# Latent attention with values as weights and probabilities scaled ahead of their transposes

## The reference

```python
def conv_attn_mixer(xn, w_in, conv_w, conv_b, conv_ln_g, conv_ln_b,
                    q_norm, kv_norm, w_uq, w_ukv, w_out):
    ...
    u = jax.nn.silu(layer_norm(u, conv_ln_g, conv_ln_b))
    ...
    q_nope, q_rope = q[..., :QK_NOPE_DIM], rope(q[..., QK_NOPE_DIM:], pos)
    kv = (rms_norm_2(c_kv, kv_norm) @ w_ukv).reshape(b, s, N_HEADS, QK_NOPE_DIM + V_HEAD_DIM)
    k_nope, v = kv[..., :QK_NOPE_DIM], kv[..., QK_NOPE_DIM:]
    k_rope = rope(k_r[:, :, None, :], pos)[:, :, 0, :]
    attn = mla_attention(q_nope, q_rope, k_nope, k_rope, v)
    return jnp.concatenate([u, attn], axis=-1) @ w_out
```

## Time and profile before

| | us |
|---|---|
| median of 3 runs | 2614.75 |
| the profiled execution, its own time | 2618.45 |
| its span, first to last instruction | 2616.0 |
| TensorE matmuls busy | 2539.7 (97%) |
| TensorE weight loads busy | 1748.8 (67%) |
| VectorE busy | 1303.1 (50%) |
| ScalarE busy | 640.2 (24%) |
| the units of the latent attention, first transposes to second half of the projection | 1553.48 to 1623.80 |

### The profile page before, as it was taken

The page is one execution under the profiler, slowest core; times in us unless marked ns, Lnnn a source line. Parts: engine busy times, 40 slices in busy tenths (PEclk is TensorE's granted clock), DMA queues, the critical chain, the costliest instruction groups (busy, mean ns, idle before and its releaser), DMA issues.

```text
span 2616.0 us, 38542 instructions
## 1 busy us (share of the span) xinstructions
PE 2539.7 (97%) x15741; PEld 1748.8 (67%) x15741; DVE 1303.1 (50%) x2873; ACT 640.2 (24%) x1168; POOL 329.5 (13%) x315
## 2 busy tenths in 40 slices
PE   8999998999999999999999999999999999999998
PEld 4766756777775684444444446688864575888887
DVE  2244565757632251000035845676765675777733
ACT  1156643323430222110011144212110122121201
POOL 0222115445441400000001000000000000000000
PEclk9999999999999999999999999999999999999999
DMA  4211111111113232444413110222223212222222
GB/s 188 77 63 49 49 56 58 39 45 52 49 50 138 88 109 81 167 171 161 174 67 113 65 48 33 89 81 97 81 97 112 97 35 81 84 94 81 95 83 80
DMA packets 32520, 227.41 MB, mean 87 GB/s; under 512 B 3552, under 2 KB 4192, under 8 KB 6112
## 3 DMA queue, kind: packets, MB, share of 16 engines
q1 hardware_dynamic: 30384, 219.50, 23.5%
q10 hardware_dynamic: 1968, 5.51, 0.6%
HBM read 222.90 MB, written 2.10 MB: 86 GB/s over the span
## 4 chain that ended last, share of the span: by engine, by line
PE 90%; DVE 4%; ACT 3%; issue 2%; POOL 1%; DMA 0%; ACTq 0%; DVEq 0%; POOLq 0%
PE psum L404 88%; PE psum L907 1%; DVE work L1613 0%; ACT work L970 0%; PE psum L2977 0%; PE psum L2638 0%; ACT work L3031 0%; PE psum L1262 0%; ACT work L968 0%; ACT work L976 0%; ACT L976 0%; ACT work L988 0%; DVE work L1920 0%; POOL ring L1455 0%; POOL ring L1438 0%
## 5 line engine op out<-in xcount | busy, mean ns | idle before, releaser
L404 PE MATMUL psum<-hT,ring 128*128 128x256 f32 (+2 forms) x2872 | 542.8, 370 | 4.0 <-issue 1.7
L404 PEld LDWEIGHTS psum<-hT,ring 128*128 128x128 f32 (+1 forms) x2872 | 371.9, 161 | 135.7 <-issue 94.0
L404 PE MATMUL psum<-work,ring 128*128 128x256 f32 (+1 forms) x1176 | 378.0, 472 | 4.6 <-ACT work L3903 2.4
L404 PEld LDWEIGHTS psum<-work,ring 128*128 128x128 f32 x1176 | 222.0, 190 | 144.3 <-issue 121.6
L404 PE MATMUL psum<-xT,ring 128*128 128x256 f32 (+2 forms) x1184 | 293.1, 400 | 15.6 <-POOL ring L1438 7.1
L404 PE MATMUL psum<-work,mixT 128*128 128x256 f32 (+2 forms) x1332 | 289.3, 379 | 1.2 <-DVE mixT L4118 0.7
L404 PEld LDWEIGHTS psum<-work,mixT 128*128 128x128 f32 (+1 forms) x1332 | 232.1, 182 | 47.7 <-issue 16.3
L404 PE MATMUL psum<-work 32*32 32x32 f32 (+8 forms) x5374 | 255.5, 248 | 8.4 <-issue 3.7
L404 PEld LDWEIGHTS psum<-work 32*32 32x32 f32 (+5 forms) x5374 | 210.5, 124 | 78.0 <-issue 51.9
L404 PEld LDWEIGHTS psum<-xT,ring 128*128 128x128 f32 (+1 forms) x1184 | 211.0, 188 | 71.2 <-issue 25.7
L404 PE MATMUL psum<-ring,work 128*128 (+1 forms) x568 | 247.0, 593 | 0.6 <-DVE work L3198 0.6
(11 more groups left out here) (498 smaller groups left out, 2757.1 us busy)
## 6 DMA issues: line engine op xcount, KB each, us to landing
ring<-stream_dram SPq DMA_DIRECT2D x204, 1024.0 KB, 4.8
con<-consts_dram SPq DMA_DIRECT2D x1, 2953.0 KB, 13.5
mixT<-x_dram ACTq DMA_DIRECT2D x4, 512.0 KB, 6.6
work<-x_dram ACTq DMA_DIRECT2D x4, 512.0 KB, 6.3
out_dram<-mixT SPq DMA_DIRECT2D x4, 512.0 KB, 3.6
work<-p_dram ACTq DMA_DIRECT2D x1, 512.0 KB, 6.0
con<-ssm_dram ACTq DMA_DIRECT2D x1, 512.0 KB, 3.6
vec<-vecs_dram SPq DMA_DIRECT2D x1, 378.0 KB, 5.9
```

Source lines behind the costliest of these rows:

```text
L404: ins = self.eng.matmul(out, lhsT, rhs, start=start, stop=stop)
```

## The change

Three things are changed in the latent attention. Probabilities are multiplied with the reciprocal of their row sums on VectorE (`shares`), in place, ahead of their transposes; TensorE waits for that where it waited for the exponentials. The values become the weights of the last matmul and the transposed probabilities move, so that the result is 64 features by 128 tokens: a pair of heads fills the 128 partitions of one bank, a column block for each query block. With the result in that layout its transposes go, and VectorE copies a finished pair from its bank to `catT` (`pair_out`) once in 8 units. The early output projection stays at 32 matmuls: four ahead, one in each unit to unit 25, two after the last unit.

```diff
-        v_tok, o_tok2 = a(NB, T), mixT[:, DC:DC + NB, :]
+        v_tok = a(NB, T)
...
-        HALF_FIRST, HALF_LAST, TURN_AT = 4, 27, (12, 20, 28)
+        HALF_FIRST, HALF_LAST = 4, 25
...
-            def turned(self, e, c):
-
-                o = self.open(e)
-                four_of(e, o, c).then_inc(S["aux_done"], 1)
...
+        def unit_bank(e, pair):
+
+            return acc[:, (e.c["tile"].n + pair) % 2, :]
...
                 for k in range(4):
                     if m == 0 and k >= 2:
-                        e.eng.wait_ge(S["aux_free"], aux.opened + k - 3)
+                        e.eng.wait_ge(S["unit_out"], SO_FAR + k + 1)
...
             for u, (h, b) in enumerate(UNITS):
-                e.eng.wait_ge(S["probs"], SO_FAR + u + 1)
+                e.eng.wait_ge(S["shares"], SO_FAR + u + 1)
                 for k in range(b + 1):
                     ins = e.eng.transpose(blk(psum[:, 4 + u % 2, :], k), blk(m_pr[:, u % 2, :], k), ident)
                 ins.then_inc(S["turned"], 1)
                 if u + 2 < len(UNITS):
                     scores(u + 2)
-                if u in TURN_AT:
-                    aux.turned(e, TURN_AT.index(u))
                 if u <= HALF_LAST:
                     aux.half_out(e, 1)
                 e.eng.wait_ge(S["turned_a"], TURNED + u + 1)
-                if u >= 2:
-                    e.eng.wait_ge(S["unit_out"], SO_FAR + u - 1)
+                if u >= 16 and u % 8 == 0:
+                    e.eng.wait_ge(S["unit_out"], SO_FAR + u // 8 - 1)
+                o = unit_bank(e, h // 2)[VD * (h % 2):VD * (h % 2) + VD, :]
                 for k in range(b + 1):
-                    ins = e.mm(acc[:, u % 2, 0:VD], blk(m_pt[:, u % 2, :], k), v_tok[:, k, VD * h:VD * h + VD], k == 0, k == b)
+                    ins = e.mm(blk(o, b), v_tok[:, k, VD * h:VD * h + VD], blk(m_pt[:, u % 2, :], k), k == 0, k == b)
                 ins.then_inc(S["mixed"], 1)
-            e.eng.wait_ge(S["unit_out"], SO_FAR + len(UNITS))
-            aux.turned(e, 3)
+            aux.half_out(e, 4 * DC - aux.mms)
...
+            def shares(u):
+                n, d = P * (UNITS[u][1] + 1), u % 2
+                e.eng.wait_ge(S["probs"], SO_FAR + u + 1)
+                nc.vector.reciprocal(m_inv[:, d, :], m_den[:, d, :]).then_inc(S["dve_chain"], 1)
+                e.eng.wait_ge(S["dve_chain"], e.c["dve_chain"].next())
+                nc.vector.tensor_scalar(m_pr[:, d, 0:n], m_pr[:, d, 0:n], m_inv[:, d, :], None, ALU.mult)\
+                    .then_inc(S["shares"], 1)
+
+            def pair_out(pair):
+                e.eng.wait_ge(S["mixed"], SO_FAR + 8 * pair + 8)
+                nc.vector.tensor_copy(catT[:, 4 + pair, :], unit_bank(e, pair)).then_inc(S["unit_out"], 1)
 
             maxima(0)
             maxima(1)
-            for u, (h, b) in enumerate(UNITS):
-                e.eng.wait_ge(S["turned"], TURNED + u + 1)
-                nc.vector.reciprocal(m_inv[:, u % 2, :], m_den[:, u % 2, :]).then_inc(S["dve_chain"], 1)
-                e.eng.wait_ge(S["dve_chain"], e.c["dve_chain"].next())
+            shares(0)
+            for u in range(len(UNITS)):
                 if u + 2 < len(UNITS):
                     maxima(u + 2)
+                if u + 1 < len(UNITS):
+                    shares(u + 1)
                 if u == 0:
                     aux_x(0)
                 if u % 4 == 3 and u <= HALF_LAST:
                     aux_x(1 + u // 4)
-                if u in TURN_AT:
-                    aux_turned(TURN_AT.index(u))
-                e.eng.wait_ge(S["mixed"], SO_FAR + u + 1)
-                nc.vector.tensor_scalar(o_tok2[:, b, VD * h:VD * h + VD], acc[:, u % 2, 0:VD], m_inv[:, u % 2, :], None,
-                                        ALU.mult).then_inc(S["unit_out"], 1)
-                e.eng.wait_ge(S["unit_out"], SO_FAR + u + 1)
-            aux_turned(3)
-            e.eng.wait_ge(S["aux_free"], 12)
+                if u >= 8 and u % 8 == 0:
+                    pair_out(u // 8 - 1)
+            pair_out(3)
+            aux_x(DC - 1)
+            e.eng.wait_ge(S["aux_free"], DC)
```

More of the change, by code:

```diff
@@ L3218, in aux_x @@
             def aux_x(m):
[L3219 to L3226, removed]
+                e.eng.wait_ge(S["aux_done"], m + 1)
+                nc.vector.tensor_tensor(xT[:, m, :], xT[:, m, :], aux_banks[m % 2], ALU.add).then_inc(S["aux_free"], 1)
+            def shares(u):
[8 more added lines that the diff above has]
+                nc.vector.tensor_copy(catT[:, 4 + pair, :], unit_bank(e, pair)).then_inc(S["unit_out"], 1)
             maxima(0)
             maxima(1)
-            for u, (h, b) in enumerate(UNITS):
-                e.eng.wait_ge(S["turned"], TURNED + u + 1)
-                nc.vector.reciprocal(m_inv[:, u % 2, :], m_den[:, u % 2, :]).then_inc(S["dve_chain"], 1)
-                e.eng.wait_ge(S["dve_chain"], e.c["dve_chain"].next())
+            shares(0)
+            for u in range(len(UNITS)):
                 if u + 2 < len(UNITS):
                     maxima(u + 2)
+                if u + 1 < len(UNITS):
+                    shares(u + 1)
                 if u == 0:
```

## The result

The changed kernel takes 2636.36 us (median of 4 runs, 2630.04 to 2640.32) where the kernel before takes 2615.2 (2613.24 to 2618.49): a ratio of 1.0069, 95% interval 1.0056 to 1.0081. A second series gave 2633.0 (2631.06 to 2636.11), ratio 1.0069 (1.0047 to 1.009). So it is slower, by 17 to 21 us; the forecast was 2626, with 2634 as its upper end. The profiled execution of after is the fastest of its runs, 2630.04 with a span of 2628.2.

A forecast was written before the change was run, and what follows sets the result against it. TensorE was taken to bound the kernel, fully busy in the changed stretch. +9.1 us up to unit 26 and +2.4 in the tail made +11.5; against the median 2614.75 that gave 2626 us, range 2618 to 2634.

The forecast's parts named there:

- the ring: Units' loop: scores(u+2), maxima(u+2), shares(u+1), TensorE's transposes of u+1; one unit's slack where two were; waits of 1.40 us a head.
- the result transposes: Latent attention: 16 transposes at 0.107 us go; two groups of 0.43 lie in the busy stretch, -0.86 us.
- The tail: Units 26 to 31 and the last two half_outs, mostly without cover: 15.10 us instead of 12.66, +2.4.
- Value matmuls: Latent attention: 80 matmuls of two passes turn round; 128 moving columns priced at 0.107 a pass, +0.14 us a head.
- The upper bound that the step kept: 160 value passes, 0.05 us more each if truly twice as long: about 8 us in all.
- the refill of 0.17: TensorE's restart after waiting for the scaling: 0.17 us, taken between 0.11 and 0.23.
- The 0.66 of the earlier trace: Kernel before: four transposes after a wait take 0.66 us to the next matmul; a stream takes 0.43, so 0.23 refill.
- the forecast's constant 0.87: Fixed steps after the scores' end; plus maximum of u+2 and scaling of u+1, compared with half_out 0.86 plus 0.214 x k.
- The prediction's own sign: Profile after: TensorE waits for scaling before transposes of units with k (key blocks) = 3, 2, 4, not k = 1.
- The scaling's price: VectorE's scaling ahead of the transposes: 0.28, 0.35, 0.42, 0.48 us for 128 to 512 columns.
- Covered ring: Rival: half_out covers the loop's waits, none left in the busy stretch; about 2613.7 us, chance 0.11.
- The clock: TensorE's clock should hold in the heads; rival: falls in each head, about +10 us, 2636, chance 0.06.

The follow-up runs named there:

- second series: The changed kernel measured once more, nothing altered, against the kernel before: 2633.0 us, ratio 1.0069.
- wide weights: Changed kernel with values as full 128-column weights, a bank and copy for each head: 2629.18 us; with shares(u+1) also ahead of maxima(u+2): 2623.23 us.
- Without the stops: Changed kernel with 61 already satisfied waits, 30 instructions, added to TensorE's stream ahead of the attention: 2625.08 us, ratio 1.0038.
- Both tests: Satisfied waits added to TensorE's stream: in the changed kernel 2625.08 us, stops gone; in the kernel before (195 instructions) 2620.24 us, both stops present.

## Why the prediction was right, and where it was not

The side was right, and the attention's own loss nearly exact: +11.1 us where +11.5 had been summed. That agreement is luck: two large errors cancel, and one term of the loss was in no step. Up to unit 26 the forecast had +0.9 for the values, +9.0 for the ring and -0.9 for the result transposes. The kernel without scaling takes 65.33 there, 7.7 more than the 57.66 before, so the values cost 7.7 + 0.86 = 8.5. From there to the 67.06 of after it is 1.7, of which the ring makes some 0.6 (0.09 a head) and one scaling beside GpSimd 1.1 (last section). The tail adds 1.7. Another part of the loss, in the state-space stage, was not in the sum at all.

- **Value matmuls: the term that was mis-sized.** +0.14 a head was taken; without any ring they cost +1.33, which is 0.19 for the longer passes and 1.14 for the narrow weights. The step took the 0.107 of the transposes as the nearest row, and looked only at the pace within a group. With 128-column weights it is nearly right (8.92 - 8.73 = 0.19). It did not ask whether a load of 64 columns still runs ahead of the matmuls before it. The loss comes with each switch, twice in a unit: 0.09 into the values, 0.18 from their start to the next transposes (0.05 of it the longer passes), 0.06 at the transposes, 0.33 x 4 units. The upper bound that the step kept, 8 us in all, is near the 8.5 measured up to unit 26, but was argued for another reason: it is 160 times half of the row's 0.107, not worked out from a figure of the Trainium skill.
- **The ring: right in kind, too long by 0.3.** VectorE in the unit with k = 1 of the profile after; the scores end at 1595.31 and the next load starts at 1596.71:

```profile
1595.52 0.42 DVE L3203 CUSTOM_DVE_ANT_0 work<-psum,work 128x256 f32<-128x256 f32 x1 [0.83 <-issue]
...
1595.98 0.15 DVE L3207 TENSOR_SCALAR work<-work 128x1 f32<-128x1 f32 x1
1596.05 0.15 DVE L3216 RECIPROCAL work<-work 128x1 f32<-128x1 f32 x1
1596.24 0.42 DVE L3218 TENSOR_SCALAR work<-work 128x384 f32<-128x384 f32 x1
```

  It is 1.40 long instead of 1.71. The scores' end to the maximum is 0.21, not 0.34, and the refill of 0.17 hardly shows: from 1596.71 three transposes take 0.39 where a stream takes 0.32. The 0.66 of the earlier trace rows was taken for a price at full clock, but 0.30 of it lies behind 1623.50, where the earlier trace rows has the clock at 0.50. The other steps are as summed. With 0.56 for the forecast's constant 0.87, its own formula gives waits of 0, 0.33, 0.10 and 0.04 a head, 0.47 in all. Measured with wide weights, ring against no ring, it is 9.53 to 9.63 less 8.92, 0.6 to 0.7, not 1.40. In the changed kernel itself it is hidden but for 0.1. The prediction's own sign would have told: TensorE was to wait for the scaling ahead of three units in four, and waits ahead of one.
- **The scaling's price** held: 286 ns for 128 columns (mean of 8), 420 for 384, and 353 and 486 for 256 and 512 where GpSimd is still.
- **Result transposes** (-0.86) and the copies went as said. **The tail** was +1.7, not +2.4: the ring there is shorter too.
- **Covered ring:** the rival was right that the ring hardly shows (0.1 a head), but not in its time and not in its reason: the slow weights hide the ring, and with wide weights it shows.
- **The clock:** full in all heads, as forecast. In the profiled run a fall was added in the state-space stage and one behind the tail went.
- **What no step had:** the length of TensorE's code. 61 instructions fewer cost 3.8 us of stops in the profile, and in some runs a fall of the clock behind them; 8 us lie between the medians of the two kernels. Without the stops the change measures 1.0038, some 2625 against the base of the forecast, 1 us from it. With them the median of the first series, 2636, lies past the forecast's upper end of 2634; the second series (2633) and the ratio (1.0069 x 2614.75 = 2633) lie just inside it.

## What to carry to other kernels

Price a matmul that is turned round not only by its passes but by its switches: see in the weight loads' rows whether each load still starts ahead of its matmul, and keep the column width of neighbouring weights alike. Two causes that bind the same loop need not add: here both together gave little more than the longer one alone. So take each away alone and both together before naming one. Where a loss appears in a stage that wasn't touched and TensorE stops for no semaphore, count instructions to the stop: a few empty ones ahead of it may take it away.

## What the runs showed of the hardware that was not expected

- Loads of 64-column weights between loads of 128 columns are not taken ahead of the running matmuls, nor is the next load of 128 columns (1593.69 and 1594.70 in the rows above, against 0.43 and 0.11 ahead with equal widths): 0.28 us for each pair of switches, with 0.05 of longer passes beside it. Whether it is the width or the place in the output that decides was not tried.
- TensorE stopped for 1.5 to 2.5 us at two counts of its instructions, in seven of the eleven profiles. Both tests show that the count decides. That fetching code is the cause, and the load of 1 MB what holds it up, is read from the traces and was not tried apart: in all 14 stops TensorE goes on 1.2 to 1.6 us after the end of a code packet that came only with the end of a load, and in the four profiles without stops the packet starts ahead of the load or with it.
- In after the scaling of unit 15 took 1.61 us instead of 0.35, the next one 0.68 instead of 0.49, and that head 11.26 us instead of 10.15. GpSimd was multiplying just then (VectorE, then GpSimd):

```profile
1587.90 1.61 DVE L3218 TENSOR_SCALAR work<-work 128x256 f32<-128x256 f32 x1
...
1590.86 0.68 DVE L3218 TENSOR_SCALAR work<-work 128x512 f32<-128x512 f32 x1
...
1587.46 3.80 POOL L3414 TENSOR_TENSOR ring<-ring,vec 128x1024 f32<-128x1024 f32 x2 [71.06 <-DMA ring<-stream_dram]
```

  The first of GpSimd's two ends at about 1587.46 + 1.90 = 1589.36, and the scaling 0.15 later. The Trainium skill (SBUF — State Buffer, section SBUF: two separate sides) says that the two engines share a pair of ports which one of them locks for a whole instruction while the other waits, when VectorE runs in one of its faster modes. The trace agrees in the end times, and every other profile with this scaling has one that is too long beside that multiplication (0.82 to 1.95 us), while the three without it (before, before with added instructions, no scaling) have none. It was not tried apart.
